# Second experts read whole gate and up matrices, quad 0's rows picked by products, attention gate tiles dealt anew

## What is computed

```python
s = einsum("bhqd,bhkd->bhqk", q_i, kh) * scale
s = s + c_i[..., :, None] - c[:, :, None, :]
s = where(kpos[None, :] <= qpos[:, None], s, -inf)
o = einsum("bhqk,bhkd->bhqd", softmax(s), vh)
```

```python
a = einsum("nd,edf->nef", hf, w_gate)
b = einsum("nd,edf->nef", hf, w_up)
u = silu(a) * b * combine[..., None]
y = einsum("nef,efd->nd", u, w_down)
```

## Time and profile before

| | us |
|---|---|
| median of 3 runs | 1931.56 |
| lowest and highest | 1930.52, 1934.93 |
| the profiled execution, its own time | 1928.75 |
| its span (first to last instruction) | 1927.0 |

### The profile page before, as it was taken

How to read it: one execution, slowest core, us unless ns; L and a number is a source line. 1 busy time by engine, 2 the same in 40 slices (tenths; PEclk the granted TensorE clock), 3 DMA queues, 4 the chain that set the end, 5 groups by cost and what they waited for, 6 DMA issues and landing times. The chain is left out here.

```text
span 1927.0 us, 18124 instructions
## 1 busy us (share of the span) xinstructions
PE 1730.1 (90%) x6987; PEld 788.3 (41%) x6987; DVE 554.9 (29%) x1088; ACT 385.4 (20%) x700; POOL 24.0 (1%) x34
## 2 busy tenths in 40 slices
PE   6998999999989999999999899978999999457882
PEld 4544545554436443444443334423444334212220
DVE  4605403551124011101111159553110113410113
ACT  5102113431022110010100310166300112300112
POOL 0100000000000000000000000000000000100001
PEclk9998999999999999999999999989999999778996
DMA  9611364111323999999999803111112131489965
GB/s 368 240 44 44 110 218 174 45 66 46 129 87 133 409 419 423 425 421 420 421 422 425 308 2 129 44 44 44 44 44 87 54 120 66 162 253 361 306 212 182
DMA packets 97193, 383.05 MB, mean 199 GB/s; under 512 B 11284, under 2 KB 11620, under 8 KB 86628
## 3 DMA queue, kind: packets, MB, share of 16 engines
q1 hardware_dynamic: 87268, 350.14, 47.3%
q10 hardware_dynamic: 5824, 17.30, 2.9%
q0 software_dynamic: 4032, 14.68, 2.0%
HBM read 467.03 MB, written 18.87 MB: 252 GB/s over the span
## 5 line engine op out<-in xcount | busy, mean ns | idle before, releaser
L1738 PE MATMUL bank<-H,weight_slots 128*128 128x512 f32 (+1 forms) x1024 | 424.4, 575 | 4.1 <-ACT H L677 2.9
L1738 PEld LDWEIGHTS bank<-H,weight_slots 128*128 128x128 f32 x1024 | 197.4, 194 | 226.0 <-issue 220.3
L1738 PE MATMUL bank<-R,weight_slots 128*128 128x512 f32 x576 | 250.9, 594 | 4.4 <-DVE R L1285 2.1
L1738 PEld LDWEIGHTS bank<-R,weight_slots 128*128 128x128 f32 x576 | 108.4, 190 | 143.2 <-issue 133.8
L2064 PE MATMUL bank<-weight_slots,SM 128*64 128x512 f32 x640 | 143.9, 595 | 9.4 <-DMA weight_slots<-in_w_up_e 9.4
L2390 PE MATMUL bank<-weight_slots,SM 128*32 128x512 f32 x768 | 98.3, 659 | 34.2 <-DMA weight_slots<-in_expert_w_up 33.4
L2092 PE MATMUL bank<-weight_slots,SM 128*64 128x512 f32 x384 | 113.7, 604 | 3.4 <-DMA weight_slots<-in_w_down_e 3.4
L1738 PE MATMUL bank<-R 128*128 128x128 f32 (+2 forms) x720 | 95.8, 286 | 3.5 <-ACT R L964 2.0
L1738 PEld LDWEIGHTS bank<-R 128*128 128x128 f32 x720 | 87.0, 195 | 6.9 <-issue 4.4
L2064 PEld LDWEIGHTS bank<-weight_slots,SM 128*64 128x64 f32 x640 | 45.4, 137 | 104.3 <-issue 84.2
L1738 PE MATMUL bank<-weight_slots,H 128*128 128x512 f32 x192 | 82.9, 592 | 0.0
(11 more groups left out here) (419 smaller groups left out, 1525.1 us busy)
## 6 DMA issues: line engine op xcount, KB each, us to landing
weight_slots<-in_expert_w_gate SPq DMA_DIRECT2D x102, 512.0 KB
weight_slots<-in_expert_w_up SPq DMA_DIRECT2D x102, 512.0 KB
R<-in_expert_w_down SPq DMA_DIRECT2D x51, 1024.0 KB
weight_slots<-in_w_up_e SPq DMA_DIRECT2D x24, 2048.0 KB, 17.3
weight_slots<-in_w_down_e SPq DMA_DIRECT2D x24, 2048.0 KB, 23.7
weight_slots<-in_w_in SPq DMA_DIRECT2D x18, 2048.0 KB, 10.2
weight_slots<-in_w_gate_e SPq DMA_DIRECT2D x16, 2048.0 KB, 17.0
weight_slots<-in_w_ada SPq DMA_DIRECT2D x12, 2048.0 KB, 10.6
```

Source lines behind the costliest of these rows:

```text
L1738: ins = nc.tensor.matmul(dst, lhsT, rhs, start=(i == 0), stop=(i == len(pairs) - 1))
```

## The change

Four things are changed.

1. `load_half(i, 0)` now loads the whole gate matrix of a slot and `load_half(i, 1)` the whole up matrix, each as one transfer of 1 MB. `gate_up(q, 0)` runs all 8 slices of the gate, `gate_up(q, 1)` all 8 of up, in products of 256 columns: twice as many instructions, each half as wide. Loads ahead of the tables carry no condition.
2. Quad 0's rows are picked by PE: DVE builds a 0/1 matrix (`first_rows`) from the token positions, ahead of the block tables, and `pick_rows` multiplies the token rows with it, 32 products of 128 columns, in the place of `turn_rows(0)`. `load_rows(0)` falls away.
3. The gate tiles of the attention stage: PE runs gate `2 hp + 1` between the two halves of the next pair's scores and gate `2 hp + 2` behind them. Pair 3 keeps gate 7 alone. ACT empties gate 0 ahead of the exponentials of pair 1 and the others in the new order. `norm_conv` and `conv_silu` each stand one pair later.
4. The buffers that hold the loaded rows are listed in another order, so that the token rows stay in place while PE reads them.

```diff
@@ -370,12 +371,16 @@
         h2_stage = R6[:, :].rearrange("p (t d) -> p t d", t=TT)
         column, first, thresh = (const[:, CONST[n]:CONST[n] + k] for n, k in (("column", NG), ("first", NSLOT), ("thresh", T // BLK)))
+        column_row = const[:, CONST["column_row"]:CONST["column_row"] + NSLOT]
+        pos_in = R7[:, 2256:2256 + 2 * TT * NSLOT].rearrange("p (a t c) -> p a t c", a=2, c=NSLOT)
+        first_rows = R7[:, 3072:3072 + T].rearrange("p (t s) -> p t s", t=TT)
+        second_rows = R7[:, 3584:3584 + T].rearrange("p (t s) -> p t s", t=TT)
         desc = const[:, CONST["desc"]:CONST["desc"] + 4].unsqueeze(1).broadcast_to([P, TT, 4])
         xb = [SM[:, 1024 * a:1024 * (a + 1)].rearrange("p (k s) -> p k s", k=KD) for a in range(2)]
         h_flat = H[:, :, :].rearrange("p k t -> p (k t)")
         x_flat = xT[:, :, :].rearrange("p k t -> p (k t)")
         x_tok2 = h_flat[:, 0:4096].rearrange("p (t d) -> p t d", t=TT)
-        rows_in = [a[:, D * i:D * (i + 1)] for a, n in ((R5, 2), (R6, 4), (h_flat[:, 4096:6144], 2), (x_flat, 4)) for i in range(n)]
+        rows_in = [a[:, D * i:D * (i + 1)] for a, n in ((R5, 2), (h_flat[:, 4096:6144], 2), (x_flat, 4), (R6, 4)) for i in range(n)]
         sgb = R7[:, 0:FF]
         hb = R7[:, FF:2 * FF]
         hbT = R7[:, 2 * FF:3 * FF].rearrange("p (i s) -> p i s", i=2)
@@ -551,9 +556,12 @@
                 sp.dma_start(ring[:, s, :].rearrange("p (k n) -> p k n", k=src.shape[1]), src).then_inc(arrived[s], 16)
             def load_half(i, half, expert, changed=None):
-                for j, name in enumerate(("expert_w_gate_2", "expert_w_up_2")):
-                    src = A[name][0].rearrange("e (p k) n -> p e k n", p=P)[:, expert, 4 * half:4 * half + 4, :]
-                    dst = ring_jk[i][:, j:j + 1, 4 * half:4 * half + 4, :]
+                name = ("expert_w_gate_2", "expert_w_up_2")[half]
+                src = A[name][0].rearrange("e (p k) n -> p e k n", p=P)[:, expert, :, :]
+                dst = ring_jk[i][:, half:half + 1, :, :]
+                if changed is None:
+                    sp.dma_start(dst, src).then_inc(sem(f"half{half}_in"), 16)
+                else:
                     sp.dma_start(dst, src, cond=changed).then_inc(sem(f"half{half}_in"), 16)
             def load_down(i, expert, changed=None):
@@ -580,8 +588,8 @@
             load_down(3, slice(3 * EPG, 3 * EPG + 1))
             sp.dma_start(g_out, A["norm_final_g_2"].rearrange("(a n) -> a n", a=1).broadcast_to([P, D])).then_inc(sem("g_out_in"), 16)
             sp.wait_ge(*reached("block_tables", 1))
-            sp.wait_ge(sem("half0_in"), 16 * 8)
-            sp.wait_ge(sem("half1_in"), 16 * 8)
+            sp.wait_ge(sem("half0_in"), 16 * NSLOT)
+            sp.wait_ge(sem("half1_in"), 16 * NSLOT)
             sp.wait_ge(sem("down_in"), 16 * 4)
             here = [block_of_step(0, i) for i in range(NSLOT)]
             for half in range(2):
@@ -915,11 +923,14 @@
             for hp in range(FOX_H // 2):
                 if hp + 1 < FOX_H // 2:
                     cb_copy(hp + 1)
+                    if hp == 0:
+                        gate_c(0)
                     probs(hp + 1)
+                    gate_c(2 * hp + 1)
+                    gate_c(2 * hp + 2)
                 else:
                     scale_probs(FOX_H * TT - 1)
-                gate_c(2 * hp)
-                gate_c(2 * hp + 1)
+                    gate_c(2 * hp + 1)
                 for e in range(2):
                     for t in range(TT):
                         n = 8 * hp + 4 * e + t
@@ -930,7 +941,7 @@
                         act.activation(PT2[:, c:c + 512 - 128 * t], PS[6 + t % 2][:, 128 * t:512], ACT.Copy).then_inc(sem("PT_ev"), 1)
                 act.wait_ge(sem("pv2_mm"), 2 * hp + 2)
                 act.activation(q2[:, hp, :], PS[5][:, :], ACT.Copy).then_inc(sem("attn_ev"), 1)
-                if hp == 1:
+                if hp == 2:
                     conv_silu()
             for j in range(8):
                 act.wait_ge(*reached("gam", j + 1))
@@ -1032,7 +1043,7 @@
                     act.dma_start(rows_in[q][BLK * c:BLK * (c + 1), :], by_step[q, c]).then_inc(sem(f"rows_in{q % 4}"), 16)
             act.wait_ge(sem("rows_out"), 16 * 2 * TT)
-            for q in range(4):
+            for q in range(1, 4):
                 load_rows(q)
             for q in range(NQUAD):
                 if q:
@@ -1630,6 +1641,15 @@
             step(nc.vector.reduce_sum(pos2[:, 1, :], pos, AX_X))
             tt(pos2[:, 1, :], pos2[:, 1, :], pos2[:, 0, :], ALU.subtract)
             nc.vector.tensor_scalar(token_slot[:, TT:2 * TT], pos2[:, 1, :], -1.0, 0.0, ALU.add, ALU.max).then_inc(sem("token_slots"), 1)
+
+            step(nc.vector.tensor_tensor(pos_in, pos2.unsqueeze(3).broadcast_to([P, 2, TT, NSLOT]),
+                                         column_row.unsqueeze(1).unsqueeze(1).broadcast_to([P, 2, TT, NSLOT]), ALU.subtract))
+            in_block = iota[:, 0:BLK].unsqueeze(1).unsqueeze(1).broadcast_to([P, TT, NSLOT, BLK])
+            for a, rows in enumerate((first_rows, second_rows)):
+                nc.vector.tensor_tensor(rows.rearrange("p t (c r) -> p t c r", c=NSLOT), in_block, pos_in[:, a, :, :].unsqueeze(3).broadcast_to([P, TT, NSLOT, BLK]),
+                                        ALU.is_equal).then_inc(sem("first_hits"), 1)
+            dve.wait_ge(sem("first_hits"), 2)
+            nc.vector.tensor_tensor(first_rows, first_rows, second_rows, ALU.add).then_inc(sem("first_hits"), 1)
             by_column = expert_prev.rearrange("a (c q) -> a c q", c=NSLOT)
             step(nc.vector.tensor_copy(by_column[:, :, 0], first[0:1, :]))
@@ -2225,11 +2245,10 @@
                 if hp + 1 < FOX_H // 2:
                     decays(hp + 1)
                     logits(hp + 1, (0, 1))
-                    if hp == 0:
-                        gate_c(1)
+                    gate_c(2 * hp + 1)
                     logits(hp + 1, (2, 3))
-                if hp:
-                    gate_c(2 * hp)
+                    gate_c(2 * hp + 2)
+                else:
                     gate_c(2 * hp + 1)
                 pe.wait_ge(sem("P_ready"), 8 * (hp + 1))
                 out_b = take(5, "attn_ev", hp + 1)
@@ -2364,8 +2383,17 @@
                                        start=False, stop=(t == TT - 1))
             ins.then_inc(sem("rank_mm"), 1)
+            def pick_rows():
+                pe.wait_ge(*reached("h_rows", TT))
+                pe.wait_ge(sem("first_hits"), 3)
+                for i in range(2):
+                    for k in range(4):
+                        c = 128 * (4 * i + k)
+                        ins = product(PS[i][:, 128 * k:128 * (k + 1)], [(h2_stage[:, t, c:c + 128], first_rows[:, t, :]) for t in range(TT)])
+                    ins.then_inc(sem("q_turn_x"), 1)
+
             def turn_rows(q):
-                pe.wait_ge(sem(f"rows_in{q % 4}"), 16 * NSLOT * (q // 4 + 1))
+                pe.wait_ge(sem(f"rows_in{q % 4}"), 16 * NSLOT * (q // 4 + (1 if q % 4 else 0)))
                 for i in range(2):
                     if q:
                         pe.wait_ge(sem("q_xb"), 2 * (q - 1) + i + 1)
@@ -2383,11 +2411,12 @@
                 ins.then_inc(sem("q_turn_h"), 1)
             def gate_up(q, half):
-                pe.wait_ge(sem(f"half{half}_in"), 16 * (8 * (q + 2) - 2))
-                for k in range(4 * half, 4 * half + 4):
+                pe.wait_ge(sem(f"half{half}_in"), 16 * (4 * (q + 2) - 1))
+                n = slice(FF * half, FF * half + FF)
+                for k in range(KD):
                     for i in range(4):
                         r = slice(BLK * i, BLK * (i + 1))
-                        ins = nc.tensor.matmul(PS[2 + q % 2][r, :].rearrange("p (j n) -> p j n", j=2), xb[q % 2][:, k, r], ring_jk[i][:, :, k, :],
+                        ins = nc.tensor.matmul(PS[2 + q % 2][r, n], xb[q % 2][:, k, r], ring_jk[i][:, half, k, :],
                                                start=(k == 0), stop=(k == KD - 1), tile_position=(0, BLK * i))
                 ins.then_inc(sem("gate_up_halves"), 1)
@@ -2406,7 +2435,7 @@
             for name, value in (("xtok_v", 2 * TT), ("x_sq", 2 * TT), ("thin_ev", 5), ("g_v", 2), ("token_slots", 2)):
                 pe.wait_ge(*reached(name, value))
-            turn_rows(0)
+            pick_rows()
             for q in range(NQUAD):
                 pe.wait_ge(sem("q_xb"), 2 * (q + 1))
                 if q >= 2:
```

More of the change, by code:

```diff
@@ L104 @@
 SHARED = {"product_done": bases(PRODUCT_STAGES), "copy_done": bases(COPY_STAGES), "vector_done": bases(VECTOR_STAGES)}
-CONST = {"ident": 0, "ones": 128, "s_le_j": 256, "s_ge_j": 384, "future": 512, "dft": 640, "iota": 896, "pick": 960, "fold": 962, "desc": 982, "column": 986, "first": 990, "thresh": 994, "both_norms": 1010, "final_norm": 1011, "eps2": 1012}
-NCONST = 1013
```

(3 more changed lines are left out.)

## The result

The changed kernel takes 1903.23 us (median of 4 runs, 1900.17 to 1905.36) against 1933.24 for the kernel before beside it (4 runs): a ratio of 0.9842, 95% interval 0.9819 to 0.9866, so 30 us less, with 26 to 35 in the interval. 1900.6 was forecast from a median of 1931.56. Run again later beside the kernel before, the same kernel gave 1907.49 against 1934.74 (0.9849, 0.9825 to 0.9873), 27 us less.

The account below looks back on a forecast made before the run. PE, busy 90% of the span, sets the pace almost everywhere; transfers limit the second experts. Attention -19.0 and second experts -12 make -31, so 1931.56 becomes 1900.6 us; range 1891.0 to 1917.0.

Parts of the forecast that it names:

- The experts' -12: Second experts, start and rest together: 12 us less, bounds -4 and -18.
- The values of pair 0 at full clock, 8.6: Attention, pair 0: gate 2 keeps PE warm, so the values take 8.6 us, not 10.80.
- Stretches ahead of pairs 2 and 3: Attention, pairs 1 and 2 in the forecast's sums: 20.5 us each, in place of 22.00 and 28.00.
- pair 2's -7.5: Attention, pair 2: 20.5 us in place of 28.00, with conv_silu moved one pair on, 7.5 less.
- rival (a): Attention: gates with table loads among ACT's exponentials cost more, so attention gives -10, in all 1909.6 us; chance 0.18.
- the signs: Changed profile: pick_rows over by about 1664, first 256-column products at about 1672.5, gate and up idle 25 to 30 us.
- First product: Second experts, gate_up(0, 0): starts at 1691.5, not 1699.85, on the landing of the expert's gate matrix, -8.3 us.
- Quad 1: Second experts, gate_up(1, 0): at 1704.3, not 1713.45, -9.2 us; -10 with a shorter cold stretch.
- The loads, -2: Second experts behind quad 1: fewer issues and 8 KB lines shorten each load wait by 0.2 to 0.5 us, -2.
- (c): Second experts: narrow products have a floor above their columns, +0.35 us in 24 halves, in all 1909.0; chance 0.05.
- (d): Second experts, 24 halves: a product costs by its count, not its columns, +23 us, in all 1954; chance 0.04.
- Rival (b): Second experts: transfers swallow the early start, so the experts give -4, in all 1908.6 us; chance 0.09.

Follow-up runs that it names:

- e5: The changed kernel with conv_silu behind the values of pair 1 again, as before the change; 23.2 us less than the kernel before, ratio 0.9868.
- e8: The changed kernel with DVE building first_rows behind the block tables, not ahead of them; 27.9 us less than the kernel before, ratio 0.9868.
- e10: The changed kernel with the edits of e7 and e8 together; 35.6 us less than the kernel before, ratio 0.9830.
- e11: The changed kernel run once more, unaltered; 1907.49 us, ratio to the kernel before 0.9849.
- e12: The changed kernel with loads by halves of gate and up (512 KB transfers) and 512-column products, as before the change; 1914.49 us, ratio to the kernel before 0.9906.
- e3: The changed kernel with quad 0's rows fetched through DRAM again, without first_rows; 13.3 us less than the kernel before, ratio 0.9930.
- e7: The changed kernel, ACT emptying gate 2 hp + 2 behind the first half of the copies, PE taking bank 5 later; 1896.60 us, ratio to the kernel before 0.9799.

## Why the prediction was right, point by point

The time was right (1900.6 for 1903.23 and 1907.49), and the sum of -31 stands beside 27 to 30 less. That it came so near is in part luck, for the attention gave 5 us less than its term. The experts' -12 is met by the stretches: B + C + D is 243.1 in the mean of the eight profiles with the new code and 254.7 in the two with the old, -11.5. Inside it two errors cancel: quad 1 came less early than forecast, and the rest gained more. With the attention's 14.0 the stretches make 25.5; whether the 27 to 30 of the medians hold more than that stays open.

- Pair 0's values start: forecast 1.6 us earlier; measured from pair 0's first scores they start 34.45 in and not 35.81: 1.4. Right.
- The values of pair 0 at full clock, 8.6: wrong, 10.0. The step "Gate 2 fills 7.0 us of the idle 9.74, so the engine comes in warm" took the engine's work before the wait for enough; some 1.8 us of wait are left behind that gate by the sum itself, 1.91 in the trace, and the clock fell behind it. It cost 1.5 us in pair 0 and, not foreseen at all, 1.5 each in pairs 1 and 2, whose values had been at full clock: 4.5 of the 5 us that the attention falls short (-14.0 for -19.0).
- Stretches ahead of pairs 2 and 3: 20.5 forecast each, 20.57 and 20.58 measured. Ahead of the last values 8.4, measured 8.56. Right. But pair 2's -7.5 didn't need `conv_silu` out of the way: e5 shows that, with the gates in their new places, it is hidden where it stood before. Whether it was what made pair 2's 28.00 in the kernel before, no run shows.
- Attention's rival (a) at -10: not so, and what is short is the clock, not table loads in ACT's chain.
- `pick_rows`: 9.0 forecast, 9.21 measured. It is over at 1673.8, not at the 1664 of the signs, since the 4.4 us ahead of the attention and the attention's missing 5 moved it. First product: 19.6 us behind the token slots forecast, 18.5 measured; the rows through DRAM need 28.2. Right, by -9.4 for -8.3. The 2.4 us of DVE's work ahead of the tables, though, cost nothing (e8, e10): the load would land no earlier.
- Quad 1: forecast -9.2, measured 41.5 to 32.7 us behind the token slots, -8.8. Right in that profile; the mean of the eight profiles with the new code here is 34.0, that of the two with the old 40.7, so nearer to -7, where the sum had -10.
- The loads, -2 by issues and lines: mis-sized. They are worth some 7 us by e11 and e12, of which 2 to 4 us of transfer time are measured and the rest isn't split. By the means above, what stands behind quad 1 gained 4.8.
- 256-column products at 0: right, 3.64 us for 64. That is 57 ns each, so rivals (c) and (d) are out. The Trainium skill's 62 ns per product with hardware decode off ("TensorE: Matmul & The Clock Gate", section "Wait — 56ns, not 53.3ns?") is more than these rows show, so it doesn't bind here.
- The range's low end adds -21 and -18 to -40; it is -39. Nothing hangs on it.
- Rival (b), the early start swallowed: e3 speaks against it. The idle ahead of the gate and up products was forecast at 25 to 30 and is 35.1:

```profile
L2419 PE MATMUL bank<-weight_slots,SM 128*32 128x256 f32 x1536 | 99.1, 416 | 35.1 <-DMA weight_slots<-in_expert_w_gate 21.9
```

That sign was badly chosen: quad 0's wait of 6.99 now counts here, which in the kernel before stood at the turning of the rows; without it 28.1 are left. The other signs came as forecast: 1.91 us of idle ahead of the first values, 20.6 us at 1.00 ahead of pair 2's, and no idle of ACT ahead of its first exponential.

What stays open: why whole matrices gave nothing without the picked rows (e3), what part of their 7 us is due to fewer issues, why the medians of the parts add up to less than the whole, and what makes the clock fall at one place and not at the other.

## What to carry to other kernels

When filler work is put ahead of a wait, ask what is left of the wait behind the filler: behind 1.9 us of idle the values of three pairs ran partly at half clock, which took some 4.5 of the 19 us forecast, and taking the bank later and emptying the other gate later was worth more (6.5 us) than covering the idle with spare products (1.1). In a stretch that transfers pace, count engine time per byte and not bytes: 1 MB transfers with 8 KB on each partition needed 2 to 4% less of it than 512 KB ones. A transfer issued earlier may land no earlier (e8, e10): ask what else holds the transfer engines at that time.

## What the hardware showed that was not expected

- The clock fell to its lower level behind an idle of 1.91 us in front of the values (0.50 for the 3.2 us from 1299.80), and stayed at full level through the values where the idle was 1.59 or 0.73. In two kernels (e8, e12) pair 0's values took 8.5 us in spite of the same idle, so the length of the idle alone doesn't decide it.
- With that idle filled, a stretch of half clock came up in the next gate and cost 1.7 us (8.83 for 7.13) in place of 1.5. The same 8.83 stands at gate 3 in e7, where nothing was filled and the idle was 1.59, and not in e10, whose attention code is e7's.
- The stretch ahead of the attention, with identical code, varied from 1257.2 to 1264.9 us over the profiles: more than most of the single terms above.
